# NSA attention behind q's projection: one more step between scaled scores and their transposes, and q's halves summed one piece of weights later

## The reference, cut to what matters

```
s = q k^T - slope * distance            (three branches: compressed keys, selected keys, window)
p_branch = softmax(s_branch) * mask
o = gates[0] * o_cmp + gates[1] * o_slc + gates[2] * o_win
m = concat(o over heads) @ nsa_w_out
```

## The kernel before, in words

| step | TensorE | VectorE | ScalarE |
|---|---|---|---|
| 2j | scores (`ps<-l4ks,l4q`, `l4kw`, `l4kcm`) | | |
| 2j+1 | | subtract slopes, maxima (2547 to 2558) | three exponentials (1392) |
| 2j+3 | | reciprocal, scale by gate (2568 to 2575), behind the maxima of j+1 | |
| 2j+4 | transposes of the scaled scores (3444, 3445), ahead of the scores of j+2 | | |
| 2j+5 | product with the values (`ps<-l4pt,l4vs`, `l4vw`, `l4vcm`) | | copy of the transposes to `l4pt` (1382, 1384), ahead of the exponentials of j+2 |
| 2j+6 | | | copy of the result (1371) |

## Time and profile before

### The profile page before, as it was taken

How to read it: one execution, slowest core, us unless ns; L and a number is a source line. 1 busy time by engine, 2 the same in 40 slices (tenths; PEclk the granted TensorE clock), 3 DMA queues, 4 the chain that set the end, 5 groups by cost and what they waited for, 6 DMA issues and landing times.

```text
span 3363.1 us, 40637 instructions
## 1 busy us (share of the span) xinstructions
PE 3318.6 (99%) x16752; PEld 2802.4 (83%) x16752; DVE 1984.3 (59%) x2605; ACT 1570.3 (47%) x2166; POOL 59.8 (2%) x62
## 2 busy tenths in 40 slices
PE   9999999999999999999999999999999999999998
PEld 8888888888889888878888888888888788888887
DVE  5875665565766857664444444564667654444555
ACT  4573454454553545454444443453455544444443
POOL 0000000000001010000000000000000000000000
PEclk9999999999999999999999999999999999999999
DMA  6455445455443434455555555555323555555544
GB/s 255 163 197 197 166 146 198 163 200 186 179 164 126 150 126 160 152 180 186 193 193 196 192 188 188 183 209 183 135 99 116 199 186 185 194 186 200 189 177 160
DMA packets 83352, 592.50 MB, mean 176 GB/s; under 512 B 9248, under 2 KB 9760, under 8 KB 12512
## 3 DMA queue, kind: packets, MB, share of 16 engines
q1 hardware_dynamic: 80880, 576.24, 46.8%
q0 software_dynamic: 2288, 13.67, 1.1%
HBM read 587.77 MB, written 2.10 MB: 175 GB/s over the span
## 4 chain that ended last, share of the span: by engine, by line
PE 94%; DVE 3%; ACT 1%; issue 1%; DMA 0%; POOL 0%; SPq 0%; POOLq 0%; DVEq 0%; ACTq 0%
PE ps L2657 92%; DVE wlo L1470 1%; PE ps L3469 1%; DVE l L2287 0%; ACT whi L644 0%; PE ps L2807 0%; PE ps L3444 0%; ACT sq L654 0%; DVE xres L1752 0%; DVE xx L1606 0%; DVE l L1832 0%; DVE l L1833 0%; DMA col<-in_col 0%; PE ps L2897 0%; DVE xx L1493 0%
## 5 line engine op out<-in xcount | busy, mean ns | idle before, releaser
L1470 DVE TENSOR_TENSOR wlo<-raw,whi 128x1024 fp32r<-128x1024 f32 x1091 | 1309.9, 1220 | 880.1 <-ACT whi L644 878.9
L2657 PE MATMUL ps<-whi,xx 128*128 128x512 f32 x5184 | 1653.5, 394 | 7.4 <-DVE xx L1606 5.9
L644 ACT ACTIVATE whi<-raw 128x1024 fp32r<-128x1024 f32 x1091 | 1131.8, 1055 | 910.1 <-PE ps L2657 803.6
L2657 PEld LDWEIGHTS ps<-whi,xx 128*128 128x128 f32 x5184 | 974.4, 188 | 212.3 <-issue 7.7
L2657 PE MATMUL ps<-wlo,xx 128*128 128x512 f32 x2592 | 1010.1, 390 | 0.0
L2657 PE MATMUL ps<-xx,whi 128*128 128x512 f32 (+3 forms) x2464 | 781.5, 375 | 2.9 <-DVE xx L1493 2.7
L2657 PE MATMUL ps<-xx,wlo 128*128 128x256 f32 x2160 | 606.0, 281 | 0.0
L2657 PEld LDWEIGHTS ps<-wlo,xx 128*128 128x128 f32 x2592 | 487.8, 188 | 95.5
L2657 PEld LDWEIGHTS ps<-xx,whi 128*128 128x128 f32 (+2 forms) x2464 | 439.0, 186 | 88.4 <-DVE wlo L1470 3.5
L2657 PEld LDWEIGHTS ps<-xx,wlo 128*128 128x128 f32 x2160 | 404.7, 187 | 3.2 <-issue 1.9
L2657 PE MATMUL ps<-whi,fhh 128*128 128x512 f32 x704 | 274.7, 390 | 0.0
(11 more groups left out here) (355 smaller groups left out, 1686.0 us busy)
## 6 DMA issues: line engine op xcount, KB each, us to landing
raw<-in_ffn_gu SPq DMA_DIRECT2D x176, 1024.0 KB, 4.8
raw<-in_ffn_down SPq DMA_DIRECT2D x88, 1024.0 KB, 4.8
raw<-in_ab_in SPq DMA_DIRECT2D x64, 1024.0 KB, 4.8
raw<-in_ev_in SPq DMA_DIRECT2D x63, 1024.0 KB, 4.8
raw<-in_od_in SPq DMA_DIRECT2D x48, 1024.0 KB, 4.8
raw<-in_nsa_in SPq DMA_DIRECT2D x40, 1024.0 KB, 4.8
raw<-in_ev_out SPq DMA_DIRECT2D x16, 1024.0 KB, 4.7
raw<-in_od_out SPq DMA_DIRECT2D x16, 1024.0 KB, 4.8
```

The source lines that it names most:

```text
L644: self.e.activation(m.hi[i % NSPLIT][:, 0:w], m.raw[t % NRAW][:, off:off + w], ACT.Copy).then_inc(*self.up("hi", i))
L1470: self.e.tensor_tensor(m.lo[i % NSPLIT][:, 0:w], m.raw[t % NRAW][:, off:off + w], m.hi[i % NSPLIT][:, 0:w].bitcast(F32), SUB).then_inc(*se ...
L2657: return self.e.matmul(out, l, r, start=start, stop=stop, skip_group_check=True)
```

## The change

- On TensorE and ScalarE everything from the transposes on moves one step later: transposes of j at step 2j+5, their copy and the product with the values at 2j+6, the copy of the result at 2j+7. Scores, maxima, exponentials and scaling keep their steps. So on ScalarE the copy of the transposes of j now stands behind the exponentials of j+2, where it stood ahead of them. On TensorE an even step now holds a product with the values and then scores, an odd step holds transposes.
- The rate behind q becomes (3, 2), as it is already under `nsa_out`.
- From block 1 of q on, VectorE sums each half of q after the split and the ticks of one further piece. The first `nsa_out` part takes one piece fewer in exchange.

```diff
-R4 = ((7, 5), (3, 2))
+R4 = ((3, 2), (3, 2))
...
     def proj(self, n_tiles):
-        for _ in range(2 * n_tiles):
+        self.half_tiles(2 * n_tiles)
+
+    def half_tiles(self, n):
+        for _ in range(n):
             self.ahead()
             self.tick()
             self.used += 1
...
# Scalar.attention4
-            if t >= 6 and t % 2 == 0 and (t - 6) // 2 < 32:
-                it = (t - 6) // 2
+            if t >= 7 and t % 2 == 1 and (t - 7) // 2 < 32:
+                it = (t - 7) // 2
...
-            if t >= 5 and t % 2 == 1 and (t - 5) // 2 < 32:
-                it = (t - 5) // 2
+            if t >= 6 and t % 2 == 0 and (t - 6) // 2 < 32:
+                it = (t - 6) // 2
...
# Vector.layer4
-        for i in range(4):
-            self.pair_block([m.l4_q[:, i * 4 + 2 * q:i * 4 + 2 * q + 2, :] for q in range(2)], "l4_q", i, SQ)
+        q_half = lambda i, q: self.evict_pair(m.l4_q[:, i * 4 + 2 * q:i * 4 + 2 * q + 2, :], "l4_q", i, q, SQ)
+        for q in range(2):
+            self.proj(2)
+            q_half(0, q)
+        self.f.add(("q", 0))
+        self.half_tiles(1)
+        for i in range(1, 4):
+            for q in range(2):
+                self.half_tiles(3)
+                if (i, q) == (3, 1):
+                    self.rate = R4[1]
+                    self.heads(0)
+                self.half_tiles(1)
+                q_half(i, q)
             self.f.add(("q", i))
-        self.rate = R4[1]
...
# Tensor.attention4: values at 2j+6 (was 2j+5), transposes at 2j+5 (was 2j+4)
-            if t >= 5 and t % 2 == 1 and (t - 5) // 2 < 32:
-                it = (t - 5) // 2
+            if t >= 6 and t % 2 == 0 and (t - 6) // 2 < 32:
+                it = (t - 6) // 2
...
-            if t >= 4 and t % 2 == 0 and (t - 4) // 2 < 32:
-                it = (t - 4) // 2
+            if t >= 5 and t % 2 == 1 and (t - 5) // 2 < 32:
+                it = (t - 5) // 2
```

More of the change, by code:

```diff
@@ L1364, in attention4 @@
         m, e = self.m, self.e
-        for t in range(32 * 2 + 5):
-            if t >= 6 and t % 2 == 0 and (t - 6) // 2 < 32:
-                it = (t - 6) // 2
+        for t in range(32 * 2 + 6):
+            if t >= 7 and t % 2 == 1 and (t - 7) // 2 < 32:
+                it = (t - 7) // 2
                 h, qt = it // 2, it % 2
@@ L1726, in add, with out_part @@
         self.e.tensor_tensor(xs, b.t, xs, ADD).then_inc(*self.up("out", tag, part, nb, tt, frees=[b]))
-    def out_part(self, tag, part, ks, dst=None, last=False, first=True, norm=None, gpost=None, loaded=None, held=False):
+    def out_part(self, tag, part, ks, dst=None, last=False, first=True, norm=None, gpost=None, loaded=None, held=False,
+                 taken=0):
         for nb in range(2 if held else 4):
-            self.proj(len(ks))
+            self.half_tiles(2 * len(ks) - (0 if nb else taken))
             if dst is None or not first:
@@ L2498, in layer4 @@
             self.out_part("nsa_out", n, [n], dst=m.l4_m, last=n == 3, first=n == 0, norm="m4", gpost=m.l4_gpost,
-                          loaded="l_gbc4", held=n == 3)
+                          loaded="l_gbc4", held=n == 3, taken=int(n == 0))
         self.boundary("nsa_out", 3, (2, 3), m.l4_m, "m4", m.l4_gpost, "l_gbc4", "l4", "x5", "norm12")
@@ L2530, in attention4 @@
         dm = m.l4_dm
-        for t in range(32 * 2 + 5):
-            if t >= 6 and t % 2 == 0 and (t - 6) // 2 < 32:
-                self.f.add(("o", (t - 6) // 2))
+        for t in range(32 * 2 + 6):
+            if t >= 7 and t % 2 == 1 and (t - 7) // 2 < 32:
+                self.f.add(("o", (t - 7) // 2))
             if t >= 1 and t % 2 == 1 and (t - 1) // 2 < 32:
```

## The result

The changed kernel takes 3379.71 us (median of 5 runs, 3379.18 to 3380.29), the kernel before 3366.68 beside it (5 runs, 3365.61 to 3366.83): 13.0 us slower, ratio 1.0041, 95% interval 1.003 to 1.0052. The forecast was +5.1 us (3371.6), the range 3359 to 3381. The sign and the mechanism came as forecast; the size is that of the second rival (3379.6). By the prediction's own line of 6.7 us this counts as slower, to which it gave 0.40, and not as no measurable change, to which it gave 0.50.

The account below looks back on a forecast made before the run. TensorE, busy 99% of the span, was taken as the bound. New waits of 12.5 us less 7.4 given back make +5.1 net, 3370.0 against the profiled execution and 3371.6 us from the median; range 3359 to 3381.

Parts of the forecast that it names:

- the second rival: Signals and TensorE's restart add 0.3 us per attention window, and the clock falls once: +13.1 us, 3379.6; chance 0.22.
- no measurable change: Whole kernel: a difference under 0.2% (6.7 us) either way, given 0.50.
- What the change gives back: Attention: two TensorE stops at transposes 5.2 us, the clock behind one 1.7, small gaps about 0.5; 7.4 us gained.
- Costs without a wait: Matmuls, copies, sums, DMA and weight stream: same work, so 0, with bounds of -1 to +1 us.
- The wait that comes instead: TensorE's value products wait for ScalarE's copy, now behind the exponentials: 12.5 us in some 16 waits.
- The need: From scores' end through exponentials and copy: 2.88 us even, 3.85 odd; in long windows 3.83 and 4.80.
- Lateness behind q: VectorE's late q sums delay the next scores in short windows by 0.83 or 1.32 us; waits behind q sum to 6.1.
- odd and even short windows: Odd or even j; short windows have two half pieces between scores and product (j divisible by 3), long ones three.
- The cover: TensorE's own path from scores' end to the product: short 3.21 even, 3.44 odd; long 4.6 even, 4.85 odd.
- the fourth: Rival on the clock: each of 8 waits of about 1 us or more loses 1.7 us, +13.6 more, 3385; chance 0.04.
- The full gain: Rival: ScalarE's copies come in time because VectorE and ScalarE run further ahead; -7.4 us, 3359.1; chance 0.16.
- That it doesn't do what it says: Rival: VectorE remains late for the transposes and half of the 7.4 us stays; 3375.3; chance 0.08.

Follow-up runs that it names:

- Three kernels in which nothing new waits: Changed kernel with ScalarE's copy ahead of the exponentials, 3357.84 us; that with q's sums in their old place, 3357.23; kernel before with only rate (3, 2), 3358.58.
- The kernel with the copy first: Changed kernel with ScalarE's copy of the transposes one step earlier, ahead of the exponentials again; 3357.84 us, ratio 0.9977.
- The doubled copy: ScalarE's first copy of the transposes made twice into the same place: on the changed kernel 3391.27 us, on the kernel before 3366.4 us.

## Why the prediction was right, and where it was not

- **What the change gives back (7.4 us): right.** Both stops at the transposes went, and with them the fall of the clock. Three kernels in which nothing new waits (3357.2 to 3358.6) lie 7.2 to 8.5 us below the kernel before.
- **Costs without a wait (0, -1 to +1): right.** The kernel with the copy first has the changed kernel's TensorE order and ends where the rate alone ends, within 0.8 us.
- **The wait that comes instead: right in place and in reason.** The need after the scores was measured as forecast: exponentials done at 2.40 us (even) and 3.15 (odd) behind an undelayed end of scores. Lateness behind q was forecast as 0.83 and 1.32 us for odd and even short windows, and measured 0.86 and 1.11.
- **The size of the waits: the term that failed, 12.5 us forecast, 16.7 measured.** Window by window, forecast and measured lateness of the product in us:

```
scores j      2    3    6    9    12   15   16   18   19   20
forecast      -    1.2  1.0  1.2  1.0  1.2  0.4  1.0  2.1  0.3
measured      1.1  2.0  1.0  1.5  1.0  1.5  0    1.0  1.9  0
scores j      21   22   23   25   26   27   29   31   5, 7, 11, 13, 17
forecast      0.45 0.25 1.0  0.2  0.45 0.45 0    0.2  0
measured      0.66 0.1  1.2  0.5  0.54 1.0  0.25 0.5  0.16 to 0.23 each
```

  The start was left out: scores 2 and 3 are taken up 1.7 and 1.4 us late, together 1.9 us above the forecast. Under the output projection scores 25, 27 and 31 are taken up 0.3 to 0.4 us late, more than I had allowed.

  Beyond that both paths were a little off in every window. The need, with VectorE on time, came out 0.07 to 0.08 us longer (behind q 2.96 for short even windows, 3.92 for short odd, 4.87 for long odd, against 2.88, 3.85 and 4.80); the 0.14 us between the end of the copy and the product, the same in every window that waits, are part of it. The cover came out 0.11 to 0.14 us shorter (short even, short odd, long even, long odd: 3.08, 3.30, 4.49 and 4.72 against 3.21, 3.44, 4.6 and 4.85), because the transposes, from their start to that of the next matmul, take 0.25 (even) and 0.46 us (odd, 2434.74 to 2435.21 in the window above) where I had estimated 0.35 and 0.58; in the kernel before, where they stand behind a product, they do take 0.33 and 0.54.

  So an odd window loses some 0.2 us more than forecast, and the long ones, whose margin was put at 0, wait 0.16 to 0.23; in short even ones VectorE's smaller lateness (1.11 against 1.32) makes up for it. The second rival said this of hand-overs alone, which are the smaller part. In windows 16 and 20 the clock was at half, which lengthened TensorE's own path enough to hide the wait.
- **The clock: a wrong reading of one row.** From a stop of 1.8 us that kept the clock I took that only longer ones lose it. In the changed kernel it fell behind a product 1.5 us late (2479) and one 1.9 us late (2510), 3.4 us in all, and did not fall behind one 2.0 us late at 2397. The second rival had one fall, the fourth eight. The length of the stop doesn't decide it alone: with the sums where they were, the product behind the same scores 19 is 1.9 us late too (at 2502), and the clock stays at 1.00. The section "A second HAM failure mode: psum-queue depth-cycling" of the Trainium skill's "TensorE: Matmul & The Clock Gate" tells of a clock that goes back and forth although the engine idles only briefly. The doubled copy agrees, where the waits are longer and more of them and the clock dips in five stretches of eleven; the run with the sums where they were and the one at the old rate have many short waits as well (8.3 us in 12 and 11.2 us in 14) and keep 1.00 throughout. What decides in a single case stays open.
- **The second rival (+13.1, slower)** took both terms: 6.3 us more for hand-overs, against 4.2 us measured above the forecast (1.9 of them at the start), and 1.7 for the clock, against 3.4. Its parts were off in opposite ways; that the total is right within 0.1 us is luck.
- **The full gain (3359.1)** is what the kernels without the new wait reach. It didn't come here for the reason named in the forecast. **That it doesn't do what it says** is ruled out: the transposes wait no more.
- **What I didn't see.** I read the 12.3 us of VectorE's waiting for q as the cause that needs the late sums. The rate alone removes the two stops as well, and so do the late sums alone but for 0.2 us. The rows alone couldn't tell a cause from a coincidence of two periods, and I laid out the ticks of the new rate only, not those of the old pipeline at the new rate.

## What to carry to other kernels

When work is moved a step later in a software pipeline, write out for each engine what now stands ahead of it in that engine's own order. Here a copy of 0.5 us with microseconds to spare slipped behind the exponentials of the next scores but one, and so became the end of a chain of three engines within two steps. Give the step that frees TensorE the first place in its engine's order, and measure a pipeline's slack for the windows with the least cover, not on the average of 20 us in which ScalarE is half idle. And try the rate before the depth: one number did here what the deeper pipeline was written for.

## What the runs showed of the hardware

The list of waits understates a short stop of TensorE: 13.1 us listed in 14 cases, 16.7 from start to start in 21. The list counts from the modelled end of the matmul ahead, which leaves out 0.17 us of each (1.31 against 1.48 in the window above), and stops under some 0.3 us don't show in it at all. The idle time of the weight load (20.7 us) overstates it, as loads run ahead. And the granted clock fell to half behind products 1.5 and 1.9 us late, each time at a cost of 1.7 us, but not behind one 2.0 us late in the same kernel, nor behind one 1.9 us late in the run with the sums where they were. The same stop of 3.4 us cost 1.7 us of clock in the trace of the kernel before and 3.4 in that with the doubled copy.
